# Scoring and ranking the first tile of a group beside its query chunks, in a two-layer trunk with product-key experts

## The chip, the cores and the metric

The kernel runs on one core of a Trainium2 chip. The metric is device time in microseconds (us), from the first to the last instruction and what the runtime adds around it. All arithmetic is float32.

## The reference, cut to what matters

Five tiles of 128 tokens (tile 0 is a prompt, tiles 1 to 4 are latent tokens) pass two layers. A layer is a mixer (linear attention and pooling in layer 0, windowed attention in layer 1) and then `peer`, a mixture of 16,384 small experts:

```python
def peer(h, w_q, keys, u, v):
    qh = (x @ w_q).reshape(T, 8, 2, 128)                 # 16 query vectors of 128 per token
    s = jnp.einsum('thcd,hcnd->thcn', qh, keys)           # 16 rows of 128 scores per token
    s1, i1 = lax.top_k(s[:, :, 0], 16)
    s2, i2 = lax.top_k(s[:, :, 1], 16)
    cand = (s1[..., :, None] + s2[..., None, :]).reshape(T, 8, 256)
    top_s, top_pos = lax.top_k(cand, 16)
    experts = ...                                        # 8 heads x 16 experts per token
    gates = jax.nn.softmax(top_s, axis=-1)
    act = jax.nn.gelu(jnp.einsum('thkd,td->thk', u[experts], x))
    return jnp.einsum('thk,thkd->td', gates * act, v[experts])
```

So each tile needs 16 rows of 128 scores per token, the 16 largest of each row with their places, the 16 best pairs per head, and then 128 experts per token, each of them one vector of `u` and one of `v` (8 KB together), fetched from memory by index.

## The kernel before, in words

The program is a chain of foreground stages and one background stream.

**Foreground.** Tiles go through in groups: p0 (the prompt tile, layer 0), s0a (tile 1, layer 0), s0b (tiles 2 to 4, layer 0), j1 (the prompt tile and tile 1, layer 1), s1b (tile 2, layer 1) and s1c (tiles 3 and 4, layer 1). Behind its mixer each group runs an output stage, then `query_stage` (L1656), then `select_stage` (L1699) once for each of its tiles. Groups of one tile go through `first_experts` (L2409), the others through `other_experts` (L2425). A stage ends in `meet` (L159): TensorE, ScalarE, VectorE and SyncE each drain and wait until all four have arrived. No stage overlaps the next on these four engines.

`query_stage` works through 16 chunks (two for each head). TensorE multiplies a chunk of `w_q` with the transposed tokens in 8 matmuls (L1679) into one of two slots of PSUM, so that chunk n waits for the eviction of chunk n - 2; ScalarE evicts it into `qT` (L1687); VectorE only waits for the chunk and does background work. `select_stage` first has TensorE compute the 16 score rows (L1728), and VectorE ranks them in five passes over 16 rows: `max` (8 largest, L1754), `max_index` (L1756), `match_replace` (L1758, which takes them out), `max` again (L1760) and `max_index` again (L1762). A cast (L1770), the pairs, a ranking of eight rows of 60 candidates, and six wide operations of 2048 columns follow.

**Background.** `Experts` (L1825) does 1280 slots: 10 pairs of layer and tile with 128 slots each. For a slot, GpSimd issues an indirect DMA (L1889) of 128 rows of 8 KB (1.049 MB) into a ring of eight buffers; VectorE takes the dot product (L1897); ScalarE weighs it; and the weighted `v` row is added either by VectorE (`add_row`, L1906) or by TensorE with a diagonal matrix (`sum_rows`, L1932). Only the adding frees the ring buffer, and GpSimd waits for that. After 128 slots a tile is turned (L1981 to L1985, L1942, L1950, and zero matmuls at L1961).

**What sets the order.** Every stage has a number of units and a rate. `tick` (L203) puts background slots behind unit u of the foreground until slot base + int(u x rate) is reached, and the stage's end aligns all engines at base + int(units x rate). `lead` slots are done ahead of the first unit. Which engine adds a slot comes from the rate's second field: all eight ring places on TensorE in a select stage (`PE_8`), none in a query stage (`PE_0`). ScalarE and TensorE run one and three slots behind VectorE. What is not done in a stage is done later: in `finish` (L2058) at two barriers, and in `tiles` (L2113) at the very end, both in loops with five places on TensorE. In p0 the same mechanism drives `Early` instead, 40 steps that prepare the latent tiles (L2309); here the query rate is 0, and `early.finish` does what is left.

The query stage has 16 units and the select stage 21. The rates (slots a unit, places on TensorE, lead):

```python
EARLY  "query": (0.0, None, 0), "select": (0.6, None, 1)
FIRST  "query": (1.0, PE_0, 2), "select": (0.8, PE_8, 3)                                        # s0a
REST   "query": (2.0, PE_0, 2), "first select": (1.5, PE_8, 3), "select": (2.1, PE_8, 3)        # s0b
JOINT  "query": (0.7, PE_0, 2), "first select": (2.0, PE_8, 3), "select": (2.1, PE_8, 3)        # j1
LATENT "query": (0.9, PE_0, 2), "first select": (2.0, PE_8, 3), "select": (2.1, PE_8, 3)        # s1b, s1c
```

Of the kernel before, what the change touches and what calls it, by code (L numbers as in the profile page):

```python
# [23 lines left out]
P = 128  # L24
# [1631 lines left out]
def query_stage(core, tag, NT, hT, qT, queries, rate=None):  # L1656
# [4 lines left out]
    with Stage(core, tag, HC, rate) as s:  # L1661
        pq = s.ps("pq", [P, 2, 512])
        q_mm, qT_done = s.sem("q_mm"), s.sem("qT_done")
# [9 lines left out]
        def _(pe):  # L1673
            for n in range(HC):
# [5 lines left out]
                mm.then_inc(q_mm, 1)  # L1680
                s.tick("tensor", pe, n + 1)

# [16 lines left out]
def select_stage(core, tag, tile, at, qT, keys, keys_in, experts, gates, rate=None):  # L1699
# [4 lines left out]
    LOW = -3.0e38  # L1704
    with Stage(core, tag, 21, rate) as s:
        rest = s.sb("rest", [P, HC, NKEYS])
        vals = s.sb("vals", [P, HC, TOPK])
        i1 = s.sb("i1", [P, HC, TOPK], U32)
# [11 lines left out]
        pscore = s.ps("pscore", [P, HC, NKEYS])  # L1720
# [4 lines left out]
        def _(pe):  # L1725
            pe.wait_ge(keys_in, 32)
            for n in range(HC):
                mm = nc.tensor.matmul(pscore[:, n, :], qT[:, n, at * P:(at + 1) * P], keys[:, n * NKEYS:(n + 1) * NKEYS], start=True, stop=True)  # L1728
            mm.then_inc(s_mm, 1)
            for u in range(21):  # L1730
                s.tick("tensor", pe, u + 1)

        @block.scalar
        def _(act):
            for u in range(14):
                s.tick("scalar", act, u + 1)
# [4 lines left out]
        def _(dve):  # L1741
# [24 lines left out]
            dve.wait_ge(s_mm, 1)  # L1766
            top16(lambda j: pscore[:, j, :], HC, vals, i1, lambda j: rest[:, j, :])
# [641 lines left out]
def first_experts(core, tag, tile, layer, rates, ahead=None, out_slots=3, free=None):  # L2409

    bg = core.bg
    with Stage(core, f"{tag}q") as q:
        room, qT, keys, keys_in = expert_rooms(q, 1)
        with Stage(core, f"{tag}_h") as t:
# [4 lines left out]
            query_stage(core, f"{tag}_query", 1, hT, qT, queries, rates["query"])  # L2419
        if ahead is not None:  # L2420
            ahead.load()
        select_stage(core, f"{tag}_select", tile, 0, qT, keys, keys_in, bg.experts, bg.gates, rates["select"])


def other_experts(core, tag, tiles, layer, q0, rates, spare=None):  # L2425
# [4 lines left out]
    with Stage(core, f"{tag}q") as q:  # L2430
        room, qT, keys, keys_in = expert_rooms(q, NT)
        with Stage(core, f"{tag}_h") as t:
# [8 lines left out]
            query_stage(core, f"{tag}_query", NT, hT, qT, queries, rates["query"])  # L2441
        for i, t in enumerate(tiles):
            select_stage(core, f"{tag}_select{t}", t, i, qT, keys, keys_in, bg.experts, bg.gates, rates["select" if i else "first select"])
# [177 lines left out]
```

## Time and profile before

| | us |
|---|---|
| median of 3 runs | 4240.17 (4237.74 to 4243.37) |
| the profiled execution | 4248.73 |
| its span, first to last instruction | 4246.9 |
| VectorE busy | 3039.0 (72%) |
| TensorE busy | 3021.6 (71%) |
| GpSimd busy | 1628.7 (38%) |
| ScalarE busy | 1425.0 (34%) |
| read from memory | 1516.49 MB, 358 GB/s over the span |

In the rows of windows below, the columns are the stretch, its length, the busy time of PE (TensorE), PEld (its weight loads), DVE (VectorE), ACT (ScalarE) and POOL (GpSimd) with the number of records, TensorE's granted clock, the DMA engines' busy share and GB/s. A share of busy time is a mean over stages that differ. In the 40 slices of the page the DMA engines are at nine tenths or more in most slices behind the eighth; the rate of the last ones is 410 to 422 GB/s. The profile's own time is 8.6 us (0.2%) above the median of the runs.

### The profile page before, as it was taken

What the parts mean: (1) busy time and instruction counts of PE and PEld (TensorE: products, weight loads), DVE (VectorE), ACT (ScalarE), POOL (GpSimd) and SP (SyncE); (2) the same over time, 40 slices, a digit from 0 to 9 for tenths busy, and PEclk for the clock granted to TensorE, in tenths of its full rate; (3) what the DMA queues carried; (4) which work ended last, traced back from release to release, by engine and by line L of the source; (5) the groups of instructions that cost most, each with busy time, mean ns of one, the idle gap of its engine ahead of it and who ended that gap; (6) DMA issues with size and microseconds to landing.
All of it is one profiled execution on the core that took longest, in us unless ns stands there. A gap on an engine that the chain in (4) does not pass through costs nothing.

```text
span 4246.9 us, 34403 instructions
## 1 busy us (share of the span) xinstructions
PE 3021.6 (71%) x9655; PEld 1596.2 (38%) x9655; DVE 3039.0 (72%) x6138; ACT 1425.0 (34%) x4131; POOL 1628.7 (38%) x1311
## 2 busy tenths in 40 slices
PE   5699766876878744767778867767786877656665
PEld 1365352454433201423454333553454633222222
DVE  0406769878997757697768867869787787666766
ACT  1213422522233312245423333523562233232332
POOL 0001332334544424354334434334433354554553
PEclk7798877987999966878889978889888999888888
DMA  7243897889999998999989989999999999999998
GB/s 309 101 161 115 319 389 280 334 347 361 412 367 405 399 411 329 366 387 404 389 340 367 400 353 367 381 398 374 382 380 377 357 413 398 410 422 422 418 422 366
DMA packets 222312, 1521.80 MB, mean 358 GB/s; under 512 B 29758, under 2 KB 33538, under 8 KB 48823
## 3 DMA queue, kind: packets, MB, share of 16 engines
q0 software_dynamic: 187200, 1370.25, 80.3%
q1 hardware_dynamic: 34942, 149.58, 8.9%
q8 instruction: 72, 1.18, 0.1%
q14 instruction: 98, 0.80, 0.0%
HBM read 1516.49 MB, written 3.24 MB: 358 GB/s over the span
## 4 chain that ended last, share of the span: by engine, by line
PE 31%; DMA 30%; DVE 22%; issue 7%; POOL 4%; ACT 4%; DVEq 1%; PEldq 1%; SPq 0%; PEld 0%; ACTq 0%; POOLq 0%
DMA core_ring<-in_l_uv,core_experts 24%; PE sum_rows L1932 8%; DVE core_ring L1897 6%; POOL core_ring L1889 4%; DVE core_yv L1906 4%; PE sum_rows L2309 2%; PE j_in_ps L471 2%; PE s0b_query_pq L1679 1%; PE j_query_pq L1679 1%; PE s1c_query_pq L1679 1%; DMA mod_w<-in_l_w_mod 1%; DMA s0a_h_w<-in_l_peer_wq 1%; DMA s1b_h_w<-in_l_peer_wq 1%; PE s1b_in_ps L471 1%; PE s0b_out_po L610 1%
## 5 line engine op out<-in xcount | busy, mean ns | idle before, releaser
L1889 POOL DMA_INDIRECT core_ring<-in_l_uv,core_experts x1280 | 1613.9, 1261 | 2259.6 <-DVE core_yv L1906 1055.7
L1932 PE MATMUL sum_rows<-core_ring,core_diag 128*128 128x512 f32 x3092 | 1653.0, 681 | 603.1 <-ACT core_diag L1924 532.1
L1897 DVE CUSTOM_DVE_ANT_0 core_ring<-core_ring,core_hc 128x1024 f32<-128x1024 f32 x1280 | 1551.0, 1223 | 710.7 <-DMA core_ring<-in_l_uv,core_experts 482.4
L1932 PEld LDWEIGHTS sum_rows<-core_ring,core_diag 128*128 128x128 f32 x3092 | 624.8, 215 | 1554.3 <-ACT core_diag L1924 883.7
L1918 ACT ACTIVATE core_wt<-core_wt 128x1 f32<-128x1 f32 x1280 | 256.6, 200 | 1654.6 <-DVE core_wt L1897 1566.8
L1906 DVE SCALAR_TENSOR_TENSOR core_yv<-core_ring,core_wt,core_yv 128x1024 f32<-128x1024 f32 x507 | 649.4, 1281 | 13.1 <-ACT core_wt L1921 12.1
L1921 ACT ACTIVATE core_wt<-core_wt,core_gates 128x1 f32<-128x1 f32 x1280 | 376.8, 294 | 67.2
L1924 ACT ACTIVATE core_diag<-core_ident,core_wt 128x128 f32<-128x128 f32 x773 | 310.4, 402 | 25.2
L2309 PE MATMUL sum_rows<-core_ring 128*128 128x416 f32 x320 | 118.2, 529 | 5.2 <-DVEq L158 4.1
L1918 ACT ACT_TABLE_LOAD x81 | 103.9, 1283 | 5.2 <-DVEq L158 3.8
L1897 DVE DVE_READ_ACCUMULATOR2_ANT core_wt<- 128x1 f32 x1280 | 104.5, 82 | 0.0
L1679 PE MATMUL s0b_query_pq<-s0b_h_hT,s0b_h_w 128*128 128x384 f32 x256 | 84.8, 495 | 5.5 <-DVEq L158 5.5
L2309 PEld LDWEIGHTS sum_rows<-core_ring 128*128 128x128 f32 x320 | 62.0, 196 | 57.3 <-issue 57.0
L2242 POOL DMA_DIRECT2D core_ring<-in_l_w_in x5 | 2.7, 537 | 205.2 <-PE sum_rows L2309 205.2
L357 PE MATMUL mod_pm<-mod_w,mod_c_silu 128*32 128x512 f32 x192 | 45.2, 946 | 36.1 <-DMA mod_w<-in_l_w_mod 36.1
L471 PE MATMUL j_in_ps<-j_in_w,j_atth_hT 128*128 128x384 f32 x192 | 64.4, 499 | 8.0 <-DMA j_in_w<-in_l_w_in 8.0
L1679 PEld LDWEIGHTS s0b_query_pq<-s0b_h_hT,s0b_h_w 128*128 128x128 f32 x256 | 49.5, 194 | 40.6 <-issue 7.7
L1961 PE MATMUL sum_rows<-core_zero 128*128 128x128 f32 x160 | 35.7, 413 | 40.1 <-DVE core_x L1985 36.0
L1679 PE MATMUL j_query_pq<-s_att_pr,j_h_w 128*128 128x256 f32 x256 | 58.4, 393 | 5.6 <-DVEq L158 5.6
L1679 PE MATMUL s1c_query_pq<-s1c_h_hT,s1c_h_w 128*128 128x256 f32 x256 | 58.3, 392 | 5.5 <-DVEq L158 5.5
L1574 PE MATMUL s1c_attend_po<-s_att_pr,s1c_attend_pT 128*128 128x64 f32 x160 | 32.0, 349 | 38.6 <-DVE s1c_attend_pT L1632 38.5
L335 PE MATMUL mod_ps<-mod_part,core_fold 128*2 128x512 f32 x32 | 24.7, 871 | 45.2 <-DVE mod_m L320 24.9
(777 smaller groups left out, 3231.9 us busy)
## 6 DMA issues: line engine op xcount, KB each, us to landing
mod_w<-in_l_w_mod SPq DMA_DIRECT2D x16, 2048.0 KB, 11.5
core_ring<-in_l_uv,core_experts POOLq DMA_INDIRECT x1280, 11.3
core_ring<-in_l_w_mod POOLq DMA_DIRECT2D x8, 2048.0 KB, 12.0
p_in_w<-in_l_w_in SPq DMA_DIRECT2D x5, 1664.0 KB, 16.0
core_ring<-in_l_w_in POOLq DMA_DIRECT2D x5, 1664.0 KB, 10.7
p_h_w<-in_l_peer_wq SPq DMA_DIRECT2D x16, 512.0 KB, 4.5
s0a_h_w<-in_l_peer_wq SPq DMA_DIRECT2D x16, 512.0 KB, 11.6
s0b_h_w<-in_l_peer_wq SPq DMA_DIRECT2D x16, 512.0 KB, 8.4
```

The lines of the kernel that those rows point to most:

```text
L357: mm = nc.tensor.matmul(out[lo:lo + 32, :], silu[:, k, :], w[:, k, :], start=(k < 4), stop=(k >= 4))
L471: mm = nc.tensor.matmul(ps[:, i % 4, 0:chunk], hT[:, k, t * P:(t + 1) * P], w[:, n % 2, k, :], start=(k == 0), stop=(k == DK - 1))
L610: mm = nc.tensor.matmul(po[:, t % 2, n * CH:(n + 1) * CH], own(t)[:, k, :], w[n % w_slots][:, k * CH:(k + 1) * CH], start=(k == 0), stop=( ...
L1679: mm = nc.tensor.matmul(pq[:, n % 2, 0:tok], queries.chunk(n)[:, k, :], hT[:, k, :], start=(k == 0), stop=(k == DK - 1))
L1889: nc.gpsimd.indirect_dma_start(self.ring[:, r, :], None, core.a[f"l{layer}_uv"], bass.IndirectOffsetOnAxis(ap=self.experts[:, t, n:n + 1], ...
L1897: nc.vector.tensor_tensor_reduce(self.ring[:, r, 0:D], self.ring[:, r, 0:D], self.hc[:], 1.0, 0.0, ALU.mult, ALU.add, self.wt[:, r:r + 1]) ...
L1906: nc.vector.scalar_tensor_tensor(self.yv[:], self.ring[:, r, D:], self.wt[:, r:r + 1], self.yv[:], ALU.mult, ALU.add).then_inc(self.used[r ...
L1918: nc.scalar.activation(self.wt[:, r:r + 1], self.wt[:, r:r + 1], ACT.Gelu_apprx_tanh).then_inc(self.gelu_done, 1)
L1921: nc.scalar.activation(self.wt[:, r:r + 1], self.wt[:, r:r + 1], ACT.Copy, scale=gate).then_inc(self.wt_done, 1)
L1924: nc.scalar.activation(self.diag[:, r, :], self.core.env["ident"][:], ACT.Copy, scale=self.wt[:, r:r + 1]).then_inc(self.diag_done, 1)
L1932: mm = nc.tensor.matmul(self.py[:, c * 512:(c + 1) * 512], self.diag[:, r, :], self.ring[:, r, D + c * 512:D + (c + 1) * 512], start=False ...
L2309: mm = nc.tensor.matmul(self.ps[:, i % 2 * 512:i % 2 * 512 + self.CH], self.hT[:, k, t * P:(t + 1) * P], w[:, k, :], start=(k == 0), stop= ...
```

## The change

The scores of a group's first tile and their ranking move from the select stage into the query stage. TensorE computes score row n - 1 right behind the matmuls of chunk n (row 15 behind the last). VectorE ranks four rows at a time: rows 0 to 3 behind chunk 5, rows 4 to 7 behind chunk 9, rows 8 to 11 behind chunk 13 and rows 12 to 15 behind the last one. The first select stage of a group starts at the cast and has 16 units instead of 21, at the same rates; the later tiles of a group keep all five passes. The scores' PSUM tile, `vals` and `i1` live through both stages.

```diff
+LOW = -3.0e38
+ROWS_AT_ONCE = 4
+class Ranking:
+    def __init__(self, stage):
+        self.stage = stage
+        self.vals = stage.sb("vals", [P, 2 * PH, TOPK])
+        self.i1 = stage.sb("i1", [P, 2 * PH, TOPK], U32)
+        self.scored = stage.sem("scored")
+    def open_scores(self):
+        self.scores = self.stage.ps("scores", [P, 2 * PH, NKEYS])

-def query_stage(core, tag, NT, hT, qT, queries, rate=None):
+def query_stage(core, tag, NT, hT, qT, queries, ranking, keys, keys_in, rate=None, room=None):
...
+        left = s.sb("left", [P, ROWS_AT_ONCE * NKEYS])[:] if room is None else room[:, 0:ROWS_AT_ONCE * NKEYS]
+        left = left.rearrange("p (h n) -> p h n", h=ROWS_AT_ONCE)
...
         def _(pe):
+            def score(n):
+                if n == 0:
+                    pe.wait_ge(keys_in, 32)
+                pe.wait_ge(qT_done, n + 1)
+                nc.tensor.matmul(ranking.scores[:, n, :], qT[:, n, 0:P], keys[:, n * NKEYS:(n + 1) * NKEYS], start=True, stop=True
+                                 ).then_inc(ranking.scored, 1)
             for n in range(HC):
...
                 mm.then_inc(q_mm, 1)
+                if n:
+                    score(n - 1)
                 s.tick("tensor", pe, n + 1)
+            score(HC - 1)
...
         def _(dve):
+            order = Order(dve, dve_order)
+            def rank(first):
+                rows = range(first, first + ROWS_AT_ONCE)
+                dve.wait_ge(ranking.scored, first + ROWS_AT_ONCE)
+                for j in rows:
+                    x = nc.vector.max(ranking.vals[:, j, 0:8], ranking.scores[:, j, :])
+                order(x)
+                for j in rows:
+                    nc.vector.max_index(ranking.i1[:, j, 0:8], ranking.vals[:, j, 0:8], ranking.scores[:, j, :])
+                for j in rows:
+                    x = nc.vector.match_replace(left[:, j - first, :], ranking.vals[:, j, 0:8], ranking.scores[:, j, :], LOW)
+                order(x)
+                for j in rows:
+                    x = nc.vector.max(ranking.vals[:, j, 8:16], left[:, j - first, :])
+                order(x)
+                for j in rows:
+                    x = nc.vector.max_index(ranking.i1[:, j, 8:16], ranking.vals[:, j, 8:16], left[:, j - first, :])
+                order(x)
             for n in range(HC):
                 if rate:
                     dve.wait_ge(q_mm, n + 1)
                 s.tick("vector", dve, n + 1)
+                if n >= ROWS_AT_ONCE + 1 and (n - 1) % ROWS_AT_ONCE == 0:
+                    rank(n - 1 - ROWS_AT_ONCE)
+            rank(HC - ROWS_AT_ONCE)

 select_stage
-    with Stage(core, tag, 21, rate) as s:
+    UNITS = 21 if at else 16
+    with Stage(core, tag, UNITS, rate) as s:
...
-            pe.wait_ge(keys_in, 32)
-            for n in range(HC):
+            for n in range(HC if at else 0):
                 mm = nc.tensor.matmul(pscore[:, n, :], qT[:, n, at * P:(at + 1) * P], keys[:, n * NKEYS:(n + 1) * NKEYS], start=True, stop=True)
-            mm.then_inc(s_mm, 1)
-            for u in range(21):
+            if at:
+                mm.then_inc(s_mm, 1)
+            for u in range(UNITS):
                 s.tick("tensor", pe, u + 1)
...
-            dve.wait_ge(s_mm, 1)
-            top16(lambda j: pscore[:, j, :], HC, vals, i1, lambda j: rest[:, j, :])
+            if at:
+                dve.wait_ge(s_mm, 1)
+                top16(lambda j: pscore[:, j, :], HC, vals, i1, lambda j: rest[:, j, :])
```

`first_experts` and `other_experts` make one `Ranking` for each group and hand it to both stages; s0a puts `left` into a free row of `h`.

## Rows read from the trace of the kernel before

**Rows 1.** The page: each engine's busy time, share and instructions.
```profile
PE 3021.6 (71%) x9655; PEld 1596.2 (38%) x9655; DVE 3039.0 (72%) x6138; ACT 1425.0 (34%) x4131; POOL 1628.7 (38%) x1311
```

**Rows 2.** Window of the closing loops: engines' busy time, clock, DMA share, GB/s.
```profile
3660.00:3700.00 40.00, 23.03 (x40) 8.12 (x40) 27.17 (x39) 11.97 (x42) 20.55 (x17) 0.87 1.01 422
```

**Rows 3.** Windows of query stages s0a, s0b, j1 and of j1's select stage.
```profile
579.00:637.00 58.00, 37.17 (x256) 34.60 (x256) 41.96 (x53) 11.75 (x52) 20.59 (x18) 0.89 1.02 417
1034.00:1121.00 87.00, 84.80 (x256) 49.48 (x256) 74.80 (x94) 22.08 (x80) 45.69 (x33) 0.97 1.01 411
2190.00:2250.00 60.00, 58.37 (x256) 50.58 (x256) 30.61 (x39) 11.26 (x42) 12.83 (x13) 0.95 0.91 341
2250.00:2345.00 95.00, 77.30 (x176) 34.17 (x177) 91.48 (x296) 36.63 (x116) 49.22 (x38) 0.91 0.98 388
```

**Rows 4.** Timeline of VectorE in p0's select: start, length, what, idle before it.
```profile
332.95 3.26 DVE L1754 MAX8 p_select_vals<-p_select_pscore 128x8 f32<-128x128 f32 x16 [8.06 <-PE p_select_pscore L1728]
...
352.54 0.29 DVE L1770 CAST p_select_idxf<-p_select_i 128x256 f32<-128x256 uint32 x1
```

**Rows 5.** Timeline of VectorE: ranking's start and the cast in s0a and s0b.
```profile
644.76 3.26 DVE L1754 MAX8 s0a_select_vals<-s0a_select_pscore 128x8 f32<-128x128 f32 x16
...
668.94 0.29 DVE L1770 CAST s0a_select_idxf<-s0a_select_i 128x256 f32<-128x256 uint32 x1
...
1135.35 3.26 DVE L1754 MAX8 s0b_select_vals<-s0b_select_pscore 128x8 f32<-128x128 f32 x16 [0.58 <-PE s0b_select_pscore L1728]
...
1162.96 0.29 DVE L1770 CAST s0b_select_idxf<-s0b_select_i 128x256 f32<-128x256 uint32 x1
```

**Rows 6.** Timeline of VectorE in j1: two dots, ranking's start, the cast.
```profile
2253.62 1.22 DVE L1897 CUSTOM_DVE_ANT_0 core_ring<-core_ring,core_hc 128x1024 f32<-128x1024 f32 x1
...
2255.97 1.22 DVE L1897 CUSTOM_DVE_ANT_0 core_ring<-core_ring,core_hc 128x1024 f32<-128x1024 f32 x1
2257.97 3.26 DVE L1754 MAX8 j_select_vals<-j_select_pscore 128x8 f32<-128x128 f32 x16 [0.78 <-PE j_select_pscore L1728]
...
2289.03 0.29 DVE L1770 CAST j_select_idxf<-j_select_i 128x256 f32<-128x256 uint32 x1
```

**Rows 7.** Timelines at the first barrier: GpSimd's first new gather, VectorE's last dot.
```profile
1632.60 1.68 POOL L1889 DMA_INDIRECT core_ring<-in_l_uv,core_experts  x1 [7.94 <-DVE core_yv L1906]
...
1657.78 1.23 DVE L1897 CUSTOM_DVE_ANT_0 core_ring<-core_ring,core_hc 128x1024 f32<-128x1024 f32 x1 [1.25 <-DMA core_ring<-in_l_uv,core_experts]
```

**Rows 8.** Instructions on p0's ranking tile: ns min/median/max, first and last start.
```profile
L1754 DVE MAX8 p_select_vals<-p_select_pscore x16: 277/277/299, 332.9 to 335.9; 128x8 f32<-128x128 f32 x16
...
L1756 DVE FIND_INDEX8 p_select_i<-p_select_vals,p_select_pscore x16: 289/290/292, 336.3 to 340.3; 128x8 uint32<-128x128 f32 x16
```

**Rows 9.** Evictions of query chunks in s0a, s0b, s1c: first and last start.
```profile
L1687 ACT ACTIVATE s0aq_room<-s0a_query_pq x16: 277/278/279, 583.3 to 636.1; 128x128 f32<-128x128 f32 x16
...
L1687 ACT ACTIVATE s0bq_room<-s0b_query_pq x16: 470/482/491, 1042.2 to 1120.4; 128x384 f32<-128x384 f32 x16
...
L1687 ACT ACTIVATE s1cq_room<-s1c_query_pq x16: 384/384/384, 3302.7 to 3354.5; 128x256 f32<-128x256 f32 x16
```

**Rows 10.** Timeline of VectorE: last add of query stages s0b and s1c.
```profile
1127.20 1.28 DVE L1906 SCALAR_TENSOR_TENSOR core_yv<-core_ring,core_wt,core_yv 128x1024 f32<-128x1024 f32 x1
...
3355.66 1.28 DVE L1906 SCALAR_TENSOR_TENSOR core_yv<-core_ring,core_wt,core_yv 128x1024 f32<-128x1024 f32 x1
```

**Rows 11.** Groups by line: score matmuls of s1c's two tiles (two records each).
```profile
L1728 PE MATMUL s1c_select_pscore<-s1cq_room 128*128 128x128 f32 x64 | 7.6, 277 | 2.8 <-SPq L168 2.8
```

**Rows 12.** Timeline of TensorE: opening a tile's sums in s1b's query stage.
```profile
2865.72 3.78 PE L1961 MATMUL sum_rows<-core_zero 128*128 128x128 f32 x16 [4.97 <-DVE core_x L1985]
```

**Rows 13.** Timeline of TensorE in p0: queries, a step of Early, its rest.
```profile
294.02 28.85 PE L1679 MATMUL p_query_pq<-p_h_hT,p_h_w 128*128 128x128 f32 x256 [0.37 <-PEq L163]
323.48 5.85 PE L2309 MATMUL sum_rows<-core_ring 128*128 128x416 f32 x16 [0.61 <-ACTq L153]
...
332.75 56.03 PE L2309 MATMUL sum_rows<-core_ring 128*128 128x416 f32 x160
```

More of the change, by code:

```diff
@@ L1695, in _, with select_stage @@
                 s.tick("vector", dve, n + 1)
-def select_stage(core, tag, tile, at, qT, keys, keys_in, experts, gates, rate=None):
+                if n >= ROWS_AT_ONCE + 1 and (n - 1) % ROWS_AT_ONCE == 0:
+                    rank(n - 1 - ROWS_AT_ONCE)
+            rank(HC - ROWS_AT_ONCE)
+def select_stage(core, tag, tile, at, qT, keys, keys_in, ranking, experts, gates, rate=None):
     nc = core.nc
@@ L1719, in select_stage @@
         gs = s.sb("gs", [P, PH])
-        pscore = s.ps("pscore", [P, HC, NKEYS])
+        pscore = ranking.scores
         s_mm, dve_order, shifted, exp_done = (s.sem(n) for n in ("s_mm", "dve_order", "shifted", "exp_done"))
@@ L1734, in _ @@
         def _(act):
-            for u in range(14):
+            for u in range(UNITS - 7):
                 s.tick("scalar", act, u + 1)
@@ L2406, in out_weights, with first_experts @@
     return [w[:, i, :] for i in range(count)]
-def first_experts(core, tag, tile, layer, rates, ahead=None, out_slots=3, free=None):
+def first_experts(core, tag, tile, layer, rates, ahead=None, out_slots=3, free=None, left=None):
     bg = core.bg
@@ L2413, in first_experts @@
         room, qT, keys, keys_in = expert_rooms(q, 1)
+        ranking = Ranking(q)
         with Stage(core, f"{tag}_h") as t:
@@ L2418, in first_experts @@
             output_norm_stage(core, f"{tag}_out", [tile], layer, core.env["h"], hT, room, own, queries, keys, keys_in, rates["out"])
-            query_stage(core, f"{tag}_query", 1, hT, qT, queries, rates["query"])
+            ranking.open_scores()
+            query_stage(core, f"{tag}_query", 1, hT, qT, queries, ranking, keys, keys_in, rates["query"], left)
         if ahead is not None:
             ahead.load()
-        select_stage(core, f"{tag}_select", tile, 0, qT, keys, keys_in, bg.experts, bg.gates, rates["select"])
+        select_stage(core, f"{tag}_select", tile, 0, qT, keys, keys_in, ranking, bg.experts, bg.gates, rates["select"])
 def other_experts(core, tag, tiles, layer, q0, rates, spare=None):
@@ L2440, in other_experts @@
             output_norm_stage(core, f"{tag}_out", tiles, layer, core.env["h"], hT, room, own, queries, keys, keys_in, rates["out"], free)
-            query_stage(core, f"{tag}_query", NT, hT, qT, queries, rates["query"])
+            ranking.open_scores()
+            query_stage(core, f"{tag}_query", NT, hT, qT, queries, ranking, keys, keys_in, rates["query"])
         for i, t in enumerate(tiles):
-            select_stage(core, f"{tag}_select{t}", t, i, qT, keys, keys_in, bg.experts, bg.gates, rates["select" if i else "first select"])
+            select_stage(core, f"{tag}_select{t}", t, i, qT, keys, keys_in, ranking, bg.experts, bg.gates, rates["select" if i else "first select"])
             bg.allow(q0 + 2 + i)
```

9 lines of the change are left out of this document (4 added, 5 removed).

## The prediction

> **What bounds the kernel now.** The page comes first: VectorE is busy 72% of the span [rows 1], so it cannot bound everything. I then read the windows by stage. The closing loops run at 422 GB/s with a DMA share of 1.01 while VectorE is busy 27.2 of 40 us [rows 2]. A slot is 1.049 MB, so it costs 1.049 / 0.422 = 2.49 us there, and nothing but bytes matters. The query stages differ: s0a and s0b also move 417 and 411 GB/s, with VectorE busy 42.0 of 58 and 74.8 of 87 us; j1 moves 341 and has VectorE busy 30.6 of 60, with TensorE at 58.4 [rows 3]. So the query stages of j1, and of s1c which looks the same, are TensorE's, and their ring is full. The first select stage is VectorE's: 91.5 of 95 us [rows 3].
>
> This gives the question: VectorE's ranking leaves a stage that VectorE bounds and enters one with idle VectorE time. But the stage that it leaves also did background slots meanwhile, and those must be done elsewhere.
>
> **What leaves the select stages.** In p0, which has no slots, ranking 16 rows lasts 352.54 - 332.95 = 19.6 us [rows 4]. From ranking's start to the cast it lasts 24.2 us in s0a, 27.6 in s0b [rows 5] and 31.1 in j1 [rows 6]; s1b and s1c repeat j1 (31.0 and 31.1). Above 19.6 these are dots: with all adding on TensorE a slot costs VectorE 1.15. By the rates these are 4 slots in s0a (int(5 x 0.8)), 7 in s0b, 10 in each of j1, s1b and s1c. In s1b int(21 x 2.1) - int(16 x 2.1) = 11, one more dot, 1.2 us. VectorE's waits for scores go too: 0.6 in s0b, 0.8 in j1 [rows 5, 6]; elsewhere the lead slots cover the score matmuls, and they still have to be done. Removed: 24.2 + 28.2 + 31.9 + 32.2 + 31.1 = 147.6 us.
>
> **What the dropped slots cost.** 4 + 7 + 10 + 11 + 10 = 42 slots are done later; no limit of allowed tiles is met in between. Adding up units and rates, s0b's group leaves 11 slots behind, and the first barrier does 24 slots instead of 13. There the ring starts full, eight slots are ready, and VectorE bounds the start. Gathers restart at 1632.6 [rows 7]. Slot 24 is the 16th new one: 1632.6 + 16 x 2.49 + 1 = 1673.4, against a last dot now at 1657.8 [rows 7]. That is 15.6, since DMA now works where it stood still before. The ends are 11 dots (12.7) and 11 full slots (27.4). The second barrier does nothing before or after (goals 660 and 650, both beyond its 640). The other 31 slots fall to the closing loops, 31 x 2.49 = 77.2. The loops then hold two whole tiles instead of one; I take a tile's turn there as dear as the one outside that it replaces. Together 92.8 us.
>
> **What a block of four rows costs.** `max` starts every 0.2 us and `max_index` every 0.267 [rows 8]. A pass of `max` over four is 3 x 0.2 + 0.28 + about 0.04 = 0.92, one of `max_index` 3 x 0.267 + 0.07 + 0.29 + 0.04 = 1.2; the first `max_index` and `match_replace` run on without an order between them, 8 x 0.267 + 0.13 = 2.27. Block: 0.92 + 2.27 + 0.92 + 1.2 = 5.3 us, four make 21.2, against 19.6 in one piece. It cannot be under a quarter of that, 4.9; above I allow 6.3, the `max` record of 0.28 once more for each of four orders.
>
> The trace shows `max` records of 0.277 us that start 0.2 apart [rows 8]. The Trainium skill, "VectorE: DVE Perf Modes", section "The DRAIN you can't avoid", says that the next operation starts only when the pipe has emptied and that a semaphore behind each costs nothing; by that a block would be no dearer than its share of the 16-row pass, 4.9 instead of 5.3, and the sum below 5 to 8 us lower. This trace disagrees with the first half, as starts overlap, so I keep 5.3.
>
> **How much longer the query stages get.** A slot in them is dot and add, 2.35 us (2255.97 - 2253.62) [rows 6]. I follow VectorE from the end of chunk 5's matmuls: its tick, a block, four ticks, a block, four ticks, a block, two ticks, the last block.
> - s0a: chunks come every 3.5 us [rows 9] and up to 3.8 where DMA holds them, so the scores hide. Four ticks and a block are 4 x 2.35 + 5.3 = 14.7 against 15: VectorE just keeps up, but a block pushes the slots behind it, and the last add, now 2.4 us behind the last chunk, is followed by the last block and what is left of the third. 8.2.
> - s0b: chunks every 5.2 [rows 9], two slots each: 4 x 4.7 + 5.3 = 24.1 against 20.8. VectorE becomes the bound: chunk 5 is there at 1042.2 + 5 x 5.25 = 1068.5, then 4.7 + 5.3 + 18.8 + 5.3 + 18.8 + 5.3 + 9.4 + 5.3 ends at 1141.4, against 1128.5 now [rows 10]. 13.
> - j1: TensorE bounds, so its scores count: 7.6 / 32 = 0.24 each [rows 11], 0.27 with the wait, 4.1 for 15. VectorE idles half the time, so only the fourth block and a rest of the third stand alone, 5.6. Sum 9.7.
> - s1c: the same 4.1; chunks every 3.45 [rows 9], 3.7 with scores, 0.9 slots each; the last block ends 10.2 behind the last chunk, where the last add ends 2.4 behind it now [rows 9, 10]. Sum 12.
> - s1b: the weights' DMA bounds it as in s0a: 8.
>
> A wait is added too: ScalarE's eviction stands behind weighing, which waits for VectorE's dots, so a block can hold an eviction, and TensorE waits for that two chunks on. In s1c, counted from chunk 5: tick 2.35, block 7.65, dot and weighing 9.4, evicted 9.8; TensorE asks at 3 x 3.7 = 11.1. It fits by 1.3 us, and the sum holds nothing for it. Total 50.9. Below, if only the last block of each shows besides the scores of j1 and s1c: 5 x 5.3 + 8.2 = 34.7. Above, if all 20 blocks stand bare: 106 + 8.2 = 114.
>
> **Turns that move.** A tile's turn keeps VectorE from slots for 5.0 us, for which TensorE waits, and TensorE then needs 3.8 [rows 12]. With goals 10 back, the turn at slot 771 falls from s1b's query stage, which loses some 5, into its select stage, which is VectorE's and gains 5.7 with the copy: +0.7. That at slot 899 moves from s1c's output stage into its query stage; I call it even.
>
> **p0.** TensorE bounds it: the queries, then Early to 388.8 [rows 13]; its ranking was hidden altogether. The scores move and cost the same. But the query stage now ends only when the last block is ranked. Chunk pace 28.85 / 16 + 0.25 = 2.05; the third block starts at 322.7, the fourth ends at 333.3, and TensorE's next step starts at 333.9 instead of 323.5 + 3.7 = 327.2: 6.7. The select stage now ends at step 38 of 40, and a meeting of 0.6 comes between [rows 13]. Sum 7.3, from 5 to 8.
>
> **The sum.** -147.6 + 92.8 + 50.9 + 0.7 + 7.3 = +4.1 us on the profiled execution's 4248.7, that is 4253. It lies 8.6 above the median of the runs, so the same +4.1 on 4240.2 gives 4244 us. A measurement of this kernel can tell 0.2%, 8.5 us, from no change; this is less.
>
> **Rivals.** *A, the forecast, 0.38:* what ranking gives back, slots at DMA price and longer query stages take. 4244, and of its own 4232 to 4256.
>
> *B, faster, 0.27:* VectorE's idle time in the query stages takes the blocks nearly whole. 34.7 instead of 50.9, and blocks at 4.9 another 2: 4226. For it speak 29 idle us of VectorE in j1 and 16 in s0a; against it s0b, with 12 for 21 [rows 3]. The trace shows two regimes, a query stage with VectorE half idle and a select stage with it full [rows 3]. The Trainium skill, "Perfetto Trace Analysis", section "Identifying Performance Opportunities", says that interleaving regimes with different bounds may improve performance. Where the work that it displaces ends at the DMA's rate, I hold its gain to be small.
>
> *C, slower, 0.33:* in the query stages a block holds back evictions and with them TensorE. It decides from a block of 5.3 + 1.3 = 6.6 us, or when the slots behind one are late for another reason. If one block in four stands bare above my sum, 5 x 5.3 = 26: 4271. If all do, 63 more: 4307. For it: a slack of 1.3 us. Milder, the first barrier pays full slots, +11.8: 4256.
>
> *D, 0.02:* DMA has slack later and half of the 31 slots are free: 4205. Against it 422 GB/s [rows 2].
>
> From these, faster by over 0.2%: 0.27, within 0.38, slower 0.35. The range 4218 to 4272 leaves out D and the full C.
>
> **What would show it.** From the lead slots of a first select stage straight to the cast, and 31 us less of it in j1. A block of 5.3 us. s0b's query stage 13 us longer, with VectorE never idle. TensorE idle for some 6 us ahead of Early's next step in p0. The first barrier's last dot 15.6 us later from its start. 31 more slots in the loops at 2.49. I am wrong if TensorE waits for evictions behind blocks, or if the five query stages grow by under 35 or over 70 us together.

## The result, and the profile after

The changed kernel takes 4274.7 us (median of 4 runs, 4265.2 to 4278.8) against 4241.1 for the kernel before beside it (4237.7 to 4243.4). The ratio is 1.007, with a 95% interval of 1.0053 to 1.0088. It is slower by 0.7%, where 4244 had been forecast, a change too small to tell from none. The range of 4218 to 4272 was stated for a kernel before of 4240.2 us: on that base the ratio gives 4269.9 us (4262.6 to 4277.5), inside the range near its upper end, while 4274.7 itself lies 2.7 us above it. The profiled execution took 4271.5 us with a span of 4269.7, so between the two profiles the span grew by 22.8 us, less than the 33.7 between the medians: the traces below have to explain +22.8, against a forecast of +4.1. The other 11 us are spread between executions: the profiled one of the kernel before lies 7.7 us above its median and that of the changed kernel 3.2 below. No row explains them.

The page's line of the engines, to be held against [rows 1]:

```profile
PE 3004.6 (70%) x9603; PEld 1576.9 (37%) x9603; DVE 3060.4 (72%) x6151; ACT 1420.2 (33%) x4118; POOL 1614.1 (38%) x1311
```

No sum moved by more than 22 us: the work is the same, only its place changed. The windows of the changed kernel have the same columns as [rows 2, 3]: the closing loops, the query stages of s0a, s0b and j1 up to the cast, j1's first select stage, s1c's query stage and s1c's first select stage.

```profile
3800.00:3840.00 40.00, 25.98 (x40) 8.87 (x39) 27.00 (x40) 12.09 (x43) 20.08 (x17) 0.79 1.01 422
...
579.00:652.00 73.00, 41.51 (x291) 37.52 (x292) 68.30 (x189) 14.55 (x61) 28.85 (x21) 0.87 0.97 399
...
1034.00:1137.00 103.00, 81.70 (x269) 48.93 (x268) 98.50 (x228) 23.13 (x83) 48.18 (x34) 0.90 0.94 383
...
2190.00:2265.00 75.00, 64.30 (x291) 55.18 (x292) 57.00 (x175) 13.68 (x50) 16.31 (x15) 0.91 0.82 304
2265.00:2320.00 55.00, 48.15 (x97) 18.60 (x96) 51.35 (x133) 23.55 (x72) 33.90 (x25) 0.92 1.01 409
...
3251.00:3340.00 89.00, 71.55 (x324) 61.73 (x325) 69.26 (x189) 15.06 (x56) 22.05 (x19) 0.86 0.73 265
3340.00:3400.00 60.00, 51.45 (x104) 19.70 (x103) 55.14 (x142) 25.37 (x79) 32.46 (x27) 0.92 1.01 411
```

Read the last two columns. In the loops nothing changed. But the DMA share of j1's query stage fell from 0.91 to 0.82, that of s0b from 1.01 to 0.94, and s1c's stands at 0.73 (0.94 in the kernel before, 3300 to 3350 us); j1's first select stage went from 0.98 to 1.01. Where VectorE ranks, it frees no ring buffer, so a last block behind the last chunk leaves the DMA idle. The end of j1's query stage in slices of 10 us, in the changed kernel:

```profile
2250.00:2260.00 10.00, 2.31 (x12) 1.75 (x10) 9.37 (x38) 0.85 (x4) 2.62 (x2) 0.84 0.53 174
2260.00:2270.00 10.00, 7.66 (x13) 3.13 (x13) 9.84 (x19) 4.01 (x14) 5.28 (x4) 0.65 0.57 212
```

The kernel before has such a hole too, a share of 0.63 from 2240 to 2250 us, but its next two slices are at 0.91 and 1.00. And the stage that lost its ranking is now held by the DMA (1.01).

The clearest way to see where time went is a table of intervals, each from the first start of one stage's tile to the first start of the next one's (* is the last start). "Forecast" is the prediction's sum for that stretch.

```
interval (us)                                          before   after   change  forecast
start > s0a's first mixing matmul                       445.1   452.5    +7.4     +7.3
  > s0a query > s0a candidates > s0b query              589.6   571.6   -18.0    -16.0
s0b query > first candidates                            132.4   116.8   -15.6    -15.2
  > modulation's last matmul*                           440.9   441.4    +0.5      0
first barrier, to j1's norm                              66.8    95.0   +28.2    +15.6
  > j1 query                                            515.3   513.4    -1.9      0
j1 query > first candidates                             103.0    79.3   -23.7    -22.2
  > s1b query                                           516.0   518.1    +2.1      0
s1b query > s1c attention (turn 771 in it)              203.1   185.3   -17.8    -23.5
s1c attention                                           202.8   204.0    +1.2      0
s1c output and query (turn 899) > first candidates      183.3   167.4   -15.9    -19.1
s1c candidates                                          171.4   172.2    +0.8      0
loops and end                                           677.2   752.7   +75.5    +77.2
```

(s0a's -18.0 is -16.4 in query and ranking, -6.5 ahead of them and +4.9 behind.)

### The profile page after: what moved, and what is told of

Read it like the earlier page. It is cut to its first block, busy times and chain, and to the rows that moved or that the text cites. A ratio compares the mean times of both kernels' runs of the same rounds, so it can differ in the third digit from the quotient of the medians.

```text
span 4269.7 us, 34551 instructions
## 1 busy us (share of the span) xinstructions
PE 3004.6 (70%) x9603; PEld 1576.9 (37%) x9603; DVE 3060.4 (72%) x6151; ACT 1420.2 (33%) x4118; POOL 1614.1 (38%) x1311
## 4 chain that ended last, share of the span: by engine, by line
DMA 30%; PE 28%; DVE 22%; issue 8%; POOL 4%; ACT 4%; DVEq 1%; PEld 1%; PEldq 1%; SPq 1%; ACTq 0%; POOLq 0%
DMA core_ring<-in_l_uv,core_experts 26%; PE sum_rows L1984 8%; DVE core_ring L1949 5%; DVE core_yv L1958 5%; POOL core_ring L1941 4%; PE j_in_ps L471 2%; PE s1c_query_pq L1705 1%; PE j_query_pq L1705 1%; PE sum_rows L2361 1%; DMA mod_w<-in_l_w_mod 1%; PE s0b_out_po L610 1%; PE s1b_in_ps L471 1%; PE s0b_query_pq L1705 1%; PE p_in_ps L471 1%; PEld sum_rows L2361 1%
## 5 line engine op out<-in xcount | busy, mean ns | idle before, releaser
L1958 DVE SCALAR_TENSOR_TENSOR core_yv<-core_ring,core_wt,core_yv 128x1024 f32<-128x1024 f32 x520 | 666.2, 1281 | 20.8 <-ACT core_wt L1973 14.1
L2013 PE MATMUL sum_rows<-core_zero 128*128 128x128 f32 x160 | 35.9, 415 | 49.9 <-DVE core_x L2037 45.7
## 6 DMA issues: line engine op xcount, KB each, us to landing
p_in_w<-in_l_w_in SPq DMA_DIRECT2D x5, 1664.0 KB, 11.8
```

The lines of the kernel that those rows point to most:

```text
L1958: nc.vector.scalar_tensor_tensor(self.yv[:], self.ring[:, r, D:], self.wt[:, r:r + 1], self.yv[:], ALU.mult, ALU.add).then_inc(self.used[r ...
```

## The experiments

All ratios are to the kernel before, run on the same chip in the same rounds, with a 95% interval. No experiment but the two with half rows changes what is computed.

**1. Slots kept.** All first select stages do the slots that they did before.

```diff
+    rate = rate if at else (rate[0] * 21 / 16, *rate[1:])
     with Stage(core, tag, UNITS, rate) as s:
```

> The changed kernel, but each first select stage is given the slots that it had before (the rate times 21/16), so that all goals stand where they stood in the kernel before: 42 slots return from the first barrier (11) and the closing loops (31). Theory 1 (the DMA is what these slots wait for): in the changed kernel the first select stages of j1 and s1c run at a DMA share of 1.01 and that of s0b too, so a slot that comes back there costs 2.49 us as it does in the loops, and only those of s0a (share 0.83) and some of s1b (0.86) come cheaper: about +92 there against -104 (27.4 + 77) later, and the turn at slot 899 back in the output stage gives about 10: 4250 to 4258 us, ratio to before about 1.003. Rival (VectorE bounds these stages, a slot costs its dot, 1.15 us): +48 - 104 - 10, 4208 us, ratio 0.992.

Measured 4279.8 us, ratio 1.0082 (1.0062 to 1.0101). The rival (1.15 us a slot) is out by 70 us, and theory 1 was still some 25 too low. The barrier gave back 28.4 and the end 75.9, and the select stages took all of it: +27.7 from s1b's query stage to s1c's attention for 11 slots, +29.3 in j1's and +26.2 in s1c's select stages for 10 each, +21.5 from s0b's candidates on for 7. The window of its j1 select stage:

```profile
2265.00:2345.00 80.00, 66.94 (x136) 25.75 (x136) 66.96 (x160) 32.64 (x104) 46.97 (x35) 0.95 0.97 400
```

VectorE is busy 67 of 80 us there, at a DMA share of 0.97: with the ranking gone this stage is no longer VectorE's. A slot that comes back costs 2.5 to 3.1 us in these stages, no less than in the loops; only s0a's four show no cost (-0.2 us from its query stage to s0b's). Theory 1's other term failed: the turn at slot 899 is back at the place that it had in the kernel before, early in s1c's output stage, and the two stages gain 2.0 us by it and not 10 (query -11.3, output +9.3).

**2. The turn of s1c four slots earlier.**

```diff
-LATENT_RATES["attend"])          # s1c: (2.25, PE_5, 3)
+(2.375, PE_5, 3))
```

> The changed kernel, but the attention stage of s1c does four slots more (rate 2.375 instead of 2.25), so that the turn at slot 899 falls at the end of s1c's output stage, as in the kernel before, and not in its query stage. Theory 1: the turn in the query stage costs what was missed there, some 10 us, because TensorE bounds that stage, while the output stage is VectorE's with TensorE idle; four slots move from the loops to a stage at a DMA share of about 1 and cost the same there. So the query stage of s1c gets 10 us shorter, the output stage 0 to 3 longer: 4264 to 4268 us against 4274.7 for the changed kernel, ratio to before about 1.0055. Rival (a turn costs the same wherever it is, the missing 10 us are blocks and slots behind them): the query stage keeps its length, 4273 to 4277.

Measured 4266.0 us, ratio 1.0058 (1.0043 to 1.0074), against 1.007 for the changed kernel. Theory 1 holds in size, though the two intervals overlap. In the profiles s1c's query stage is 13.8 us shorter, the output stage 2.9 longer, attention 7.3 longer and the end 12.0 shorter. But the turn does not stand "as in the kernel before": its zero matmuls start 73 us into the output stage here and 19 us into it there (L2013 at 3258.0, L1961 at 3233.6). So this shows what the end of the output stage is worth as a place, not what the change cost by moving the turn; that is experiment 1's 2.0.

**3. Fewer slots alone.** The kernel before with 16 units in the first select stage and ranking still in it.

```diff
-    with Stage(core, tag, 21, rate) as s:
+    UNITS = 21 if at else 16
+    with Stage(core, tag, UNITS, rate) as s:
...
-            unit = [0]
+            unit = [UNITS - 21]
...
-                s.tick("vector", dve, unit[0])
+                if unit[0] > 0:
+                    s.tick("vector", dve, unit[0])
```

> The kernel before, with one thing of the change alone: the five steps of ranking in each first select stage do no slots (16 units instead of 21), ranking itself stays there. 42 slots move to the first barrier and the loops. Theory 1 (a slot costs its dot in a select stage that VectorE bounds, and 2.49 us at the first barrier and in the loops alike): -48 + 27.4 + 77.2 = +57, with the turns moved as in the change +65: 4298 to 4306 us, ratio 1.013 to 1.015. Rival (the select stages of before, at a DMA share of 0.96 to 0.98, are the DMA's just as much, and a slot taken from them gives back nearly 2.49): 4245 to 4255, ratio 1.002. The forecast's own terms (first barrier 15.6) would give 4286.

Measured 4301.2 us, ratio 1.0146 (1.0125 to 1.0168). Theory 1 holds: as long as ranking is in the select stage, a slot taken from it gives back only its dot, and it costs 2.5 us later. The barrier grew by 28.2 and the end by 75.9, as in the changed kernel. So the postponed slots alone cost 60 us, and scoring and ranking beside the chunks, all the rest of the change, gain about 27 (4301.2 to 4274.7). That gain is there only with the slots gone: with all slots in their places, in the kernel before and in experiment 1, the same move costs 38 us (4241.9 to 4279.8). Neither half of the change helps by itself.

**4. Eight rows at a time.**

```diff
-ROWS_AT_ONCE = 4
+ROWS_AT_ONCE = 8
```

> The changed kernel with two blocks of eight rows instead of four of four. A block is then 10.1 us (7 x 0.2 + 0.32; 16 x 0.267 + 0.13; 1.72; 2.27) and both together 20.2 instead of 21.2; the last block, which stands alone behind the last chunk, is 4.8 longer in five stages and in p0. Theory 1 (only what comes behind the last chunk counts, blocks in the middle hold nothing back): 6 x 4.8 less 5 x 1 where VectorE bounds, +20 to +28 on 4274.7: 4295 to 4303 us, ratio 1.013 to 1.015. Rival C of the prediction (a block holds back an eviction as soon as it is longer than 6.6 us): TensorE also waits behind the first block, 3 to 5 us in each of j1, s1b and s1c, 4306 to 4318. Rival (the DMA bounds and the tail is covered by the slots that are late anyway): 4272 to 4278.

Measured 4290.5 us, ratio 1.0116 (1.0097 to 1.0135), 16 us above the changed kernel: 4 below theory 1, far from the two others. Its s1c query stage on TensorE, as a timeline of which only rows with idle time before them are kept, and VectorE's first block there:

```profile
3268.66 10.01 PE L1705 MATMUL s1c_query_pq<-s1c_h_hT,s1c_h_w 128*128 128x256 f32 x32 [5.45 <-DVEq L158]
...
3289.10 3.78 PE L2013 MATMUL sum_rows<-core_zero 128*128 128x128 f32 x16 [4.76 <-DVE core_x L2037]
...
3341.99 0.49 PE L1697 MATMUL s1cq_scores<-s1cq_room 128*128 128x128 f32 x2 [0.25 <-ACT s1cq_room L1716]
```

```profile
3321.84 1.68 DVE L1727 MAX8 s1cq_vals<-s1cq_scores 128x8 f32<-128x128 f32 x8
...
3331.83 1.22 DVE L1949 CUSTOM_DVE_ANT_0 core_ring<-core_ring,core_hc 128x1024 f32<-128x1024 f32 x1
```

The block takes 9.99 us, 10.1 was worked out, and TensorE waits for no eviction behind it, only for the stage's start, the turn and the last eviction. Rival C's hold-back is not there in s1c even with blocks of 10 us: by 3341 the chunks are through, and the cost is the block behind the last one, which starts at 3343.95.

**5. Five slots more in three query stages**, on the changed kernel.

```diff
-JOINT  "query": (0.7, PE_0, 2)
+JOINT  "query": (1.0, PE_0, 2)
-LATENT "query": (0.9, PE_0, 2)
+LATENT "query": (1.2, PE_0, 2)
```

> The changed kernel with five slots more in each of the query stages of j1, s1b and s1c (rates 1.0 for 0.7 and 1.2 for 0.9), still added on VectorE; the turn at slot 899 comes back to the end of s1c's output stage by it. Theory 1 (the changed kernel loses because the DMA stands idle in these query stages: share 0.82, 0.84 and 0.73, which is 13, 12 and 24 us, while select stages and loops are full): the 15 slots fill that time, -37 in the loops, about -10 for the turn, and VectorE with 18, 15 and 20 idle us there takes 11.8 more in each with 0 to 6 of it showing: 4230 to 4248 us, ratio 0.998 to 1.002. Rival (VectorE's order of blocks and slots is what bounds these stages, each slot shows its 2.35): +35 - 37 - 10, 4262 us, ratio 1.005, no better than the kernel with the turn alone moved.

Measured 4245.3 us, ratio 1.000 (0.9988 to 1.0012): theory 1. The end is 37.0 us shorter for 15 slots; j1's query stage with ranking took 3.0 more and s1c's 7.0 less (the turn has left), while s1b's took 15.8 more.

**6. The same, with some of those slots added by TensorE.**

```diff
-REST "query": (2.0, PE_0, 2)    JOINT (1.0, PE_0, 2)    LATENT (1.2, PE_0, 2)
+REST "query": (2.0, PE_2, 2)    JOINT (1.0, PE_2, 2)    LATENT (1.2, PE_4, 2)
```

> As the one before, and in these stages some slots are added by TensorE instead of VectorE: every second of s1b and s1c, every fourth of s0b and j1. It takes 1.2 us of VectorE for each (about 9, 9, 8 and 4 slots: 11, 11, 10, 5 us) and gives TensorE its matmuls. Theory 1: where VectorE is the bound (s0b's query stage, 98.5 of 103 us busy) and in s1b, where TensorE is busy 43 of 78 us, it gains some 5 to 10 us each; in j1 and s1c TensorE bounds and it costs 3 to 8 each: within 8 us of the one before, 4225 to 4250. Rival (VectorE bounds all of them): 15 to 25 below the one before.

Measured 4259.9 us, ratio 1.0042 (1.0025 to 1.0058), 15 slower than experiment 5. Both were wrong. In the profiles j1's stage is 4.0 and s1c's 5.8 longer (TensorE's, as theory 1 had it), but s0b's is 2.6 longer too, where a gain was expected, and only s1b's is shorter (6.4). That makes 6 of the 15; the profiled spans hardly differ (4250.3 and 4251.3), so the rest is not explained.

**7. Half rows, before and after.** In both kernels the gather brings 1024 numbers instead of 2048, and dot and add read that half.

```diff
-self.ring[:, r, :], None, core.a[f"l{layer}_uv"],
+self.ring[:, r, 0:D], None, core.a[f"l{layer}_uv"].rearrange("n (two d) -> (n two) d", two=2),
```

> The kernel before with rows of half the length gathered: 1024 numbers for each token instead of 2048, and dot and add both read this half, so what is computed differs; all instructions of the engines keep their shapes and counts. A slot is then 1.25 us of DMA, and VectorE (27.2 of 40 us busy in the loops, 1.7 us a slot) is what bounds. Theory 1: the 255 slots of the loops go from 2.49 to 1.7 or 1.9 us, -150 to -200, and the stages whose DMA share is 0.98 to 1.02 give another 50 to 150: 3900 to 4040 us. Rival (DMA is not the bound outside the loops): 4040 to 4090.

> The changed kernel with the same half rows. To be held against the kernel before with half rows. Theory 1 (the change fails because the slots that it puts off and the idle DMA of the query stages are paid in bytes): with half the bytes the 42 slots cost 1.7 to 1.9 us each instead of 2.49, 71 to 80 instead of 105, and the change as a whole comes out 10 to 30 us faster than the kernel before with half rows (-147.6 + 75 + 47 + 7 = -18). Rival (what the change loses is VectorE's and TensorE's, blocks and turns in the query stages, and has nothing to do with bytes): it stays 20 to 35 us slower, as with whole rows.

Measured 3782.3 us for the kernel before (ratio 0.8912) and 3784.8 for the changed one (0.892, 0.8904 to 0.8937). Half the bytes save 461 us, and 3782 is 118 below theory 1's lowest time: the DMA held far more than the loops. And the change now costs 2.5 us in the medians instead of 33.7, and the intervals of the two ratios overlap. By the medians neither forecast is met: the gain of 18 did not come, the loss of 20 to 35 went. The profiles say less. They caught the fastest of five executions before and the slowest of five after (3772.0 and 3793.0), and their spans still differ by 21.0 us, as with whole rows (22.8). In them the end grows by 52.9 us for 31 slots (1.71 each) instead of 75.5, and the barrier by 15.8 instead of 28.2, so the 42 slots cost 68.7 instead of 103.7; but all other stretches together give back only 47.7 instead of 80.9. So it is shown that the price of a postponed slot goes with its bytes; that the whole loss does is not.

**8. Undoing it stage by stage**, with experiment 5's slots in j1 and s1c, and in s1b as long as that is changed: p0 as before; p0 and s1b as before; only j1 and s1c changed.

```diff
-        ranking = Ranking(q)
+        ranking = Ranking(q, tag not in ('p0',))     # then ('p0', 's1b'), then ('p0', 's0a', 's0b', 's1b')
```

> The kernel with five slots more in the query stages of j1, s1b and s1c (query_slots, 4245.3 us, ratio 1.000), and in p0 the ranking goes back to its select stage. Theory 1 (in p0 ranking was hidden behind TensorE's work ahead, and its last block now holds up that work): p0 becomes 7 us shorter; in the changed kernel the start of s0a's mixing came 7.4 us later and its query stage came at the same time all the same (579.5 and 580.4), but with the other variants of it 585 to 590, so most of it stays: 4237 to 4242 us, ratio 0.998 to 0.9995. Rival (s0a's first stages wait for something else and give it back): 4243 to 4247, 1.000.

> As p0_old, and in s1b too scores and ranking go back to the select stage, with its 21 units and the old rate 0.9 in its query stage. Theory 1 (the change pays only where the query stage has VectorE time and enough slots can stand beside the blocks): by the intervals of the traces s1b took 107.1 us from its query stage to the first candidates before, 98.6 in query_slots with 6 slots fewer (15 us), so it loses about 7 there; without it 4230 to 4238, ratio 0.9965 to 0.9985. Rival (each slot put off costs the same whatever is done, s1b is even): as p0_old.

> As p0_s1b_old, and s0a and s0b are as in the kernel before too: only j1 and s1c score and rank beside their chunks, with five slots more in these query stages. Theory 1: in s0 the query stages ran at a DMA share of 1.01 before, the changes there are -33 in the two stages against +25 at the first barrier and 7 in between, even: within 3 us of p0_s1b_old, 4230 to 4240, ratio 0.997 to 0.9995. Rival (s0b's ranking beside the chunks gains, VectorE and DMA both full in its stages, as forecast): 8 or more above p0_s1b_old.

Measured 4233.9 us (ratio 0.9987, 0.9975 to 1.0000), 4233.3 (0.9981, 0.9968 to 0.9993) and 4234.3 (0.9977, 0.9965 to 0.999). Undoing p0 gains 11 us by the medians and 5 by the ratios, around its 7, though the two intervals touch: theory 1. Undoing s1b gains 0.5 us by the medians and 2.5 by the ratios, which is nothing measurable, where theory 1 had 7; its time and ratio fall within the ranges that theory 1 gave all the same. Undoing s0a and s0b gains nothing either, with theory 1 and against its rival: in layer 0 the barrier went back from 94.8 to 66.6 us and s0a's and s0b's intervals up to their candidates grew by 31.2.

**9. The slots alone.** The kernel before, with the query rates of j1 and s1c as in the last one and nothing of the change.

```diff
-JOINT  "query": (0.7, PE_0, 2)
+JOINT  "query": (1.0, PE_0, 2)
-LATENT "query": (0.9, PE_0, 2)            # s1b keeps 0.9
+LATENT "query": (1.2, PE_0, 2)
```

> The kernel before with the query stages of j1 and s1c given the same five slots more that two_groups gives them, and nothing of the change: ranking stays in the select stages everywhere. It tells whether two_groups (4234.3 us, ratio 0.9977) owes its gain to the ranking beside the chunks or to the slots alone. Theory 1 (these two query stages ran at a DMA share of 0.92 and 0.94 before, 6 and 4 idle us, so about four of the ten slots find room and six cost there what they cost in the loops): -25 in the loops, +15 to +25 in the stages, 4232 to 4242 us, ratio 0.9975 to 1.000, and the change in these two stages is worth nothing measurable beyond it. Rival (the room in the query stages is made by the change, the slots alone lengthen them by 2.35 each): 4241 to 4250, ratio 1.000 to 1.002.

Measured 4205.2 us, ratio 0.9912 (0.9892 to 0.9931). This beats both kernels and everything above, and both theories were far too careful. The same window of j1's query stage, in the kernel before and in this one:

```profile
2190.00:2262.00 72.00, 69.16 (x298) 59.05 (x299) 41.42 (x64) 14.46 (x53) 18.06 (x17) 0.91 0.92 341
```

```profile
2190.00:2262.00 72.00, 67.27 (x292) 53.41 (x292) 51.35 (x84) 17.27 (x65) 22.85 (x22) 0.97 0.99 397
```

In one execution each (39.2 us apart): ten slots made the end 22.4 shorter; j1's stage grew by 2.6 for five slots and s1c's by 1.2 for five. The intervals with the turns in them shrank besides: s1b's query stage and what follows by 10.1, s1c's attention and output stages by 6.8, though nothing was changed there but the goals (5 higher), by which the turn at slot 899 falls at the end of s1c's attention stage. With the change in j1 and s1c on top (two_groups) it is 29 us slower again: j1's interval is 23.7 shorter and s1c's 16.9, but the end is 45.4 longer for 20 slots, and s1b and s1c's output stage are 10.8 and 6.0 longer, with the turns elsewhere.

## Where the prediction held and where it missed

**Right.** The mechanism: VectorE's time against slots at the DMA's rate. The loops came out at 75.5 for 77.2. The intervals of s0a, s0b and j1 from query to candidates are within 1.5 us of their sums (s0a -16.4 for -16.0), so what leaves the select stages, the slot of 2.35 and the growth of these query stages are right. Adding to each interval what was to leave the select stage, the five query stages grew by 59.0 us together, for 50.9 and inside the 35 to 70 beyond which the prediction called itself wrong; the excess is s1c's, with the turn in it. The block was worked out at 5.3 and takes 3294.90 - 3289.64 = 5.26 (timeline of VectorE in s1c):

```profile
3289.64 0.88 DVE L1727 MAX8 s1cq_vals<-s1cq_scores 128x8 f32<-128x128 f32 x4
...
3290.64 0.29 DVE L1730 FIND_INDEX8 s1cq_i<-s1cq_vals,s1cq_scores 128x8 uint32<-128x128 f32 x1
...
3291.70 0.28 DVE L1732 MATCH_REPLACE8 s1c_query_left<-s1cq_vals,s1cq_scores 128x128 f32<-128x128 f32 x1
...
3292.81 0.87 DVE L1735 MAX8 s1cq_vals<-s1c_query_left 128x8 f32<-128x128 f32 x4
...
3293.80 0.28 DVE L1738 FIND_INDEX8 s1cq_i<-s1cq_vals,s1c_query_left 128x8 uint32<-128x128 f32 x1
...
3294.90 1.23 DVE L1949 CUSTOM_DVE_ANT_0 core_ring<-core_ring,core_hc 128x1024 f32<-128x1024 f32 x1
```

The prediction held against the Trainium skill, "VectorE: DVE Perf Modes", section "The DRAIN you can't avoid", that `max` starts overlap. That is no disagreement: the same paragraph says that a next operation that is not held starts earlier.

In p0 TensorE stands 6.37 us behind the last scores; 6.7 was forecast:

```profile
325.25 1.02 PE L1697 MATMUL p0q_scores<-p0q_room 128*128 128x128 f32 x4
332.63 7.68 PE L2361 MATMUL sum_rows<-core_ring 128*128 128x416 f32 x13 [6.37 <-DVEq L158]
```

In this pair of profiles s0a gave 6.5 of it back, but experiment 8 found 5 to 11 in p0. The interval in which it was given back (s0a's mixing to its query stage) is 128 to 135 us in kernels with the same instructions there, so this is spread.

**Wrong: the first barrier**, +28.2 for 15.6, the largest single miss. The step said that the DMA "now works where it stood still before". I had taken that from a stretch of 40 us (1600 to 1640 has a share of 0.87, which mixes in 0.70 from 1610 to 1620, ahead of the barrier). In slices of 10 us the kernel before shows this, and the changed kernel behind it, from the meeting to the last dot:

```profile
1620.00:1630.00 10.00, 0.00 (x0) 0.00 (x0) 3.72 (x6) 0.19 (x1) 3.74 (x3) 0.50 1.00 412
1630.00:1640.00 10.00, 0.00 (x0) 0.00 (x0) 10.00 (x13) 2.30 (x10) 5.41 (x4) 0.50 0.88 349
1640.00:1650.00 10.00, 1.93 (x3) 0.90 (x4) 9.62 (x13) 2.39 (x9) 5.41 (x4) 0.50 1.02 425
1650.00:1660.00 10.00, 8.01 (x15) 2.74 (x13) 7.49 (x12) 4.07 (x14) 5.52 (x5) 0.84 1.01 421
```

```profile
1594.00:1604.00 10.00, 0.00 (x0) 0.00 (x0) 3.62 (x5) 0.03 (x1) 4.06 (x4) 0.50 0.99 407
1604.00:1614.00 10.00, 3.45 (x4) 1.17 (x4) 9.55 (x14) 3.26 (x12) 4.80 (x3) 0.50 0.91 366
1614.00:1624.00 10.00, 8.19 (x17) 3.01 (x16) 7.19 (x12) 3.69 (x13) 7.50 (x6) 0.95 1.02 422
1624.00:1634.00 10.00, 4.07 (x6) 1.51 (x7) 6.30 (x10) 2.43 (x9) 3.70 (x3) 0.74 1.01 420
```

The share is 0.88 to 1.02 before: only some 1.2 us of DMA were free there. While VectorE went through its ready slots, the DMA worked off gathers issued earlier. My sum counted from the issue of the first new gather, as if it landed one slot's time later; it is behind a backlog:

```profile
1605.63 1.93 POOL L1941 DMA_INDIRECT core_ring<-in_l_uv,core_experts  x1 [6.66 <-DVE core_yv L1958]
1607.87 1.19 POOL L1941 DMA_INDIRECT core_ring<-in_l_uv,core_experts  x1 [0.30 <-issue]
```

```profile
1619.10 1.23 DVE L1949 CUSTOM_DVE_ANT_0 core_ring<-core_ring,core_hc 128x1024 f32<-128x1024 f32 x1 [1.58 <-DMA core_ring<-in_l_uv,core_experts]
...
1659.95 1.23 DVE L1949 CUSTOM_DVE_ANT_0 core_ring<-core_ring,core_hc 128x1024 f32<-128x1024 f32 x1 [1.26 <-DMA core_ring<-in_l_uv,core_experts]
```

The second new gather, issued at 1607.87, is waited for until 1619.10, 11 us; from there 16 slots take 40.85, 2.55 each. Two terms of the sum were off. It had eight slots ready and slot 24 as the 16th new gather; at the meeting 366 gathers were issued and 360 dots done, so six were ready (377 and 371 in the kernel before, six as well) and slot 24 is the 18th: 2 x 2.49 = 5.0 us. And the second new gather should have landed at 1605.63 + 2 x 2.49 + 1 = 1611.6 and did at 1619.1: 7.5 us of backlog. That is 12.5 of the 12.6 missed. In sum 11 more slots cost about 11 x 2.5. That is the milder case of rival C ("full slots, +11.8", a value of 27.4 given as the upper bound), and experiments 1 and 3 repeat it (28.4 and 28.2). Half rows make it 15.8.

**The turn at slot 899, "I call it even"**: right within 2 to 3 us in the sum of two stages, wrong for each. s1c's query stage shrank by 8.6 instead of 19.1; its output stage, rid of the turn, by 7.3: together 3.2 less than forecast. The turn in s1c's query stage in the changed kernel, TensorE and then ScalarE:

```profile
3266.53 0.39 PE L1697 MATMUL s1cq_scores<-s1cq_room 128*128 128x128 f32 x2
3271.66 3.78 PE L2013 MATMUL sum_rows<-core_zero 128*128 128x128 f32 x16 [4.75 <-DVE core_x L2037]
3275.24 4.67 PE L1705 MATMUL s1c_query_pq<-s1c_h_hT,s1c_h_w 128*128 128x256 f32 x16
```

```profile
3266.72 0.38 ACT L1716 ACTIVATE s1cq_room<-s1c_query_pq 128x256 f32<-128x256 f32 x1 [4.66 <-PE s1c_query_pq L1705]
...
3279.94 0.38 ACT L1716 ACTIVATE s1cq_room<-s1c_query_pq 128x256 f32<-128x256 f32 x1 [12.41 <-PE s1c_query_pq L1705]
```

4.75 of waiting, 3.78 of zero matmuls and a slower chunk: the pace breaks by 9.5 us (13.2 between two evictions instead of 3.7). Experiment 2 gains 10.9 in the two stages by moving it to the end of the output stage. That turn was at an expensive place, but it had stood at one before, too: back there, in experiment 1, it costs the output stage 9.3 of the 11.3 that the query stage gains. Together with s1b (-17.8 for -23.5, where two executions of the same instructions differ by 5.3) the stretches with turns hold 8.9 of the miss.

12.6 + 8.9 = 21.5 of the missing 18.7; the rest, at most 2.1 a stretch, sums to -2.8.

**The rivals.** A, the forecast, is out: even 4269.9 lies above its own 4232 to 4256. B is refuted: blocks were not cheaper and the query stages did grow by their sums. C's mechanism is refuted in s1c, with blocks of 5.3 and of 10 us; in j1 TensorE is busy without a gap from 2200 to 2250 us, in five slices of 10.00. That the time came out near C's 4271 is luck; only its milder case, the barrier, happened. D is refuted at 2.4 us a slot in the loops. What I lacked was a view of the whole: I priced the idle VectorE time of a query stage at nothing, and experiment 9 shows what else it could hold, a slot for 0.2 to 0.5 us that costs 2.2 at the end. The chances, too, don't follow from the rivals: D's 4205 is a faster outcome, so they give 0.29 for faster and 0.33 for slower, not 0.27 and 0.35.

**What stays open.** How much of experiment 9's 37 us belongs to the turns is only read from intervals of one execution each; a kernel that moves the turns alone was not run, nor one with experiment 9's slots, the change in j1 and s1c and the turns where experiment 9 has them. Nor is it shown why experiment 6 lost 15 us, nor why the stretches outside barrier and end gave back less with half rows.

## What to carry to other kernels

When the DMA is the bound over most of a kernel, ask of moving an engine's work whether it makes the DMA busier; here it made it idler in the stage that took the work, and the time got longer. Compare the DMA share of the stage that gives and the stage that takes, in slices short enough (10 us here) not to mix a full and an empty stretch. Idle engine time beside a DMA with room is already worth something to the background stream: try first to put more of the stream there, which needed three numbers here and gave 0.9%. Postponed background work cost its full price later (2.2 to 2.5 us a slot), and a rare event in the stream (a tile's turn) should be placed, not left where the counts put it.

## What the runs showed of the hardware

With rows of half the length the gathers moved 321 GB/s at a DMA share of 0.92 in a stretch near the end, where whole rows move 422 at 1.01: half the bytes at a share not much lower (the kernel before with half rows, a window of 40 us).

```profile
3500.00:3540.00 40.00, 29.15 (x70) 11.70 (x69) 36.30 (x53) 16.81 (x59) 30.62 (x24) 1.00 0.92 321
```

A slot is then 1.6 to 1.7 us (0.524 MB at 321 GB/s; 52.9 us for 31 slots), where bytes alone would give 1.25 and 1.7 to 1.9 was expected with VectorE as the bound. VectorE is at 36.3 of 40 us and the DMA at 0.92, so which of the two holds a slot there isn't told apart.
